# Gates of a dense expert layer applied to two blocks at once, and built two steps sooner

## The chip, the cores and the metric

The kernel runs on one core of a Trainium2 chip. The metric is the device time of one execution in microseconds (us); lower is better. A core has a matrix engine (PE; its weight loads are listed as PEld), a vector engine (DVE), a scalar engine (ACT), a general engine (POOL, which here only issues gathers) and a queue engine (SP, which issues the plain loads). They run side by side and are held together by semaphores.

## The reference, cut to what matters

Two transformer blocks are computed one after the other on 512 tokens of width 1024. Each ends in the same kind of layer, a product-key expert layer with 128 x 128 experts, of which every token uses 8 x 16. That layer is where the change lies:

```
expert_id = ...                     # 128 of 16384 experts for a token, expert = first key * 128 + second key
gate = softmax(best_s, axis=-1)
a = einsum('pd,ped->pe', xb, expert_down[ib])
act = gelu(a, approximate=False) * gate
y = einsum('pe,ped->pd', act, expert_up[ib])
```

## The kernel before, in words

There are four tiles of 128 tokens, and each expert layer (there are two, called layer 0 and layer 1 here) treats them in two ways at the same time.

**Tiles 0 and 1 are gathered.** POOL fetches the rows of the experts that a token uses, one row (4 KB) for each of the 128 tokens at a time, so 512 KB a gather. The DVE works on four such gathers at once, a *unit*: a "u" unit takes four dot products (`score_rows`, L1840), a "v" unit adds four weighed rows (`add_rows`, L1860). There are 128 units in a layer, u and v in turn, and a v unit needs the gelu that ACT made of a u unit three places before it (L1223). The gathered rows stand in two rings of six (`ROWS`), one for u and one for v: POOL may issue a gather only when the DVE has used up the row six places before.

**Tiles 2 and 3 are dense.** All 16384 experts are computed for these 256 tokens, in 128 *blocks* of 128 experts (one first key, all second keys). For block e the PE makes the first product (L739), ACT the gelu (L1197), the DVE multiplies by the gates (*weighs* the block, L1793) and the PE makes the second product (L749), which adds up in PSUM. Both tables of a block are loaded by SP, 512 KB each, through rings of four.

**The gates** of the 256 tokens are a mostly empty matrix, built by small matmuls (L775) for a quarter of the first keys at a time: 32 blocks, 64 *batches* of four tokens. A batch needs "hits" (L1207 and L1210 on ACT) and, for every fourth batch, a "spread" of the first keys (L1770 and L1772 on the DVE, `first_keys`). After four batches ACT copies 16 tokens' gates from PSUM into the gate buffer (`copy_gates`, L1217), 16 copies a quarter. The buffer holds one quarter and is reused in place: copy m of quarter q overwrites the places of blocks 2m and 2m + 1 of quarter q - 1, and waits until these have been weighed. A quarter's first block is weighed only when all 16 copies have been made (`ga_copied`).

**The order** is written out by hand. After a stage that builds quarter 0, a loop runs over *steps* e = 0 to 127 on every engine. In step e the PE does the first product of block e + 16 (from e = 8), the second product of block e and then the batches `batches_due(e - 1)` to `batches_due(e)`. ACT makes the gelus of the units of step e - 1, the gelu of block e + 15, the hits for the PE's next step and the copies that are due. The DVE weighs block e + 3, spreads first keys, does a piece of the choice of experts for tile 1 (41 pieces, in the first 51 steps) and runs the units that `units_due(e)` allows. `unit_table` shares the units out over the steps from assumed costs of the PE and the DVE in each step.

Of the kernel before, what the change touches and what calls it, by code (L numbers as in the profile page):

```python
# [11 lines left out]
ALU = mybir.AluOpType  # L12
# [11 lines left out]
NH, TOPK, NKEY = 8, 16, 128  # L24
# [3 lines left out]
ND = len(DENSE) * P  # L28
# [6 lines left out]
WIDES = ND // WIDE  # L35
AHEAD = 16
EARLY = 24
WEIGHED = 3
ZG = 20
RING = 4  # L40
ROWS = 6
# [59 lines left out]
LATER = (QUARTERS - 1) * BATCHES  # L101


def batches_due(e):

    return 0 if e < 0 else min(LATER, 2 * e + 4 + min(4, e // 2))


def spreads_due(e):

    return 0 if e < 0 else -(-batches_due(e + 1) // 4)


def copies_due(e):

    return 0 if e < 0 else min(LATER // 4, (e + 1) // 2 + 1)


def blocks_before(n):
# [4 lines left out]
def pieces_due(e):  # L124

    return min(PIECES, (e + 1) * 5 // 6)
# [7 lines left out]
def unit_table():  # L134

    room = []
    for e in range(NKEY - 2):
        pe = 3.45 * (1 + (EARLY <= e + AHEAD < NKEY)) + 0.37 * (batches_due(e) - batches_due(e - 1))
        other = 0.61 + 1.69 * (spreads_due(e) - spreads_due(e - 1)) + 1.25 * (pieces_due(e) - pieces_due(e - 1))
        room.append((pe, other))  # L140
    share = ((4 * GROUPS - FIRST_UNITS) * 5.15 + sum(v[1] for v in room)) / sum(v[0] for v in room)
    done, table = 0.0, []
    for pe, other in room:
        done += max(0.0, share * pe - other)
        table.append(done)
    return [FIRST_UNITS + round((4 * GROUPS - FIRST_UNITS) * v / done) for v in table]


UNITS = unit_table()


def units_due(e):

    return FIRST_UNITS if e < 0 else UNITS[min(e, len(UNITS) - 1)]
# [45 lines left out]
class Seen:  # L200
# [5 lines left out]
    def next(self, sem, by=1):  # L206
        self.n[sem.name] = self.n.get(sem.name, 0) + by
        self.eng.wait_ge(sem, self.n[sem.name])


def build(nc, a, out, mod_dram, x_dram, two_pi):
    with ExitStack() as ctx:
        def sb(name, cols, dt=F32):
            return ctx.enter_context(nc.sbuf_tensor(name, [P, cols], dt))[:, :]

        def sem(name):
            return ctx.enter_context(nc.semaphore(name))
# [8 lines left out]
        hT = hT_.rearrange("p (k n) -> p k n", k=KC)  # L226
        w_ = sb("w", 2 * KC * SEC)
        wsec = [w_[:, s * KC * SEC:(s + 1) * KC * SEC].rearrange("p (k n) -> p k n", k=KC) for s in range(2)]
        big = sb("big", 64 * 256)
# [10 lines left out]
        def part(base, at_kib, kib, dt=F32):  # L240
            v = base[:, int(at_kib * 256):int((at_kib + kib) * 256)]
            return v if dt == F32 else v.bitcast(dt)
# [22 lines left out]
        hn_, x_ = [v.rearrange("p t d -> p (t d)") for v in (hn, x)]  # L265
# [17 lines left out]
        gates = [gates_.rearrange("p (a i j) -> p a j i", a=QA, i=8), gates_.rearrange("p (j i a) -> p a j i", a=QA, i=8)]  # L283
# [6 lines left out]
        zg_first = [part(x_, n, 1) for n in range(EARLY - AHEAD)]  # L290

        def zg(e):

            return zg_first[e] if e < len(zg_first) else zg_ring[(e - len(zg_first)) % ZG]

        iaT = hT[:, 7, 0:ND]
        second_no = part(hT_, 14, 0.5, BF16)
# [125 lines left out]
        blk_done, blk_gelu = sem("block_multiplied"), sem("block_gelu_ready")  # L423
        blk_ready, blk_summed = sem("block_weighed"), sem("block_summed")
# [928 lines left out]
        def _(dve):  # L1353
# [3 lines left out]
            tt, ts, stt = nc.vector.tensor_tensor, nc.vector.tensor_scalar, nc.vector.scalar_tensor_tensor  # L1357
# [363 lines left out]
            def peer(layer):  # L1721
# [61 lines left out]
                       second_no[:, n * BATCH:(n + 1) * BATCH].unsqueeze(2).to_broadcast(shape), ALU.is_equal)\  # L1783
                        .then_inc(hit_by_vector, 1)

                def weigh_block(e):
                    at = layer * NKEY + e
                    q, j = divmod(e, QA)
                    if j == 0:
                        dve.wait_ge(ga_copied, (layer * QUARTERS + q + 1) * WIDES)  # L1790
                    dve.wait_ge(blk_gelu, at + 1)
                    z = zg(e).rearrange("p (j i) -> p j i", i=8)
                    tt(z, z, gates[q % 2][:, j, :, :], ALU.mult).then_inc(blk_ready, 1)  # L1793

                chooser = tile_experts(1)
                for n in range(BATCHES):
# [3 lines left out]
                        second_keys(n)  # L1800
                    for u in range(first_units(n - 1), first_units(n)):
                        run_unit(layer, u)
                for e in range(WEIGHED):
                    weigh_block(e)
                for e in range(NKEY):
                    if e + WEIGHED < NKEY:
                        weigh_block(e + WEIGHED)
                    for m in range(spreads_due(e - 1), spreads_due(e)):
                        first_keys(1 + m // WIDES, m % WIDES)
                    for _ in range(pieces_due(e - 1), pieces_due(e)):  # L1810
                        next(chooser)
                    for n in range(units_due(e - 1), units_due(e)):
                        run_unit(layer, n)
# [10 lines left out]
            def run_unit(layer, n):  # L1824
                kind, g = unit(n)
                if kind == "u":
                    score_rows(layer, g)
                else:
                    add_rows(layer, g)
                    if g % GROUPS == GROUPS - 1:  # L1830
                        finish_tile(layer, g // GROUPS, y)
# [104 lines left out]
            for h in range(8):  # L1936
# [3 lines left out]
                for j in range(NT):  # L1940
                    n = h * NT + j
# [24 lines left out]
            for n in range(STICKS + LOOK):  # L1966
# [12 lines left out]
                if n < STICKS:  # L1979
                    h, j = n // NT, NT - 1 - n % NT  # L1980
# [13 lines left out]
                if m >= 0:  # L1994
                    h, j = m // NT, NT - 1 - m % NT
# [85 lines left out]
```

## Time and profile before

| | |
|---|---|
| median of 3 runs | 3348.59 us (3344.89 to 3349.8) |
| profiled execution, its own time | 3350.17 us |
| profiled execution, span from first to last instruction | 3348.4 us |
| PE, DVE, ACT, POOL busy | 92%, 74%, 39%, 40% |
| granted clock of the matrix engine, mean | 0.961 |
| steps 0 to 127 of layer 0 | about 710 to 1644 us |
| steps 0 to 127 of layer 1 | about 2402 to 3338 us |

The busy shares are means over stages with different limits, so the steps have to be read by themselves. Times inside the profile count from the span's start. Durations of neighbouring DVE instructions overlap slightly (a start can lie some 0.08 us before the end of the one before).

### The profile page before, as it was taken

What the parts mean: (1) busy time and instruction counts of PE and PEld (TensorE: products, weight loads), DVE (VectorE), ACT (ScalarE), POOL (GpSimd) and SP (SyncE); (2) the same over time, 40 slices, a digit from 0 to 9 for tenths busy, and PEclk for the clock granted to TensorE, in tenths of its full rate; (3) what the DMA queues carried; (4) which work ended last, traced back from release to release, by engine and by line L of the source; (5) the groups of instructions that cost most, each with busy time, mean ns of one, the idle gap of its engine ahead of it and who ended that gap; (6) DMA issues with size and microseconds to landing.
All of it is one profiled execution on the core that took longest, in us unless ns stands there. A gap on an engine that the chain in (4) does not pass through costs nothing. (4 is left out here: it accounts for less than half of the span.)

```text
span 3348.4 us, 46062 instructions
## 1 busy us (share of the span) xinstructions
PE 3096.9 (92%) x16440; PEld 2061.0 (62%) x16440; DVE 2462.3 (74%) x5627; ACT 1311.1 (39%) x3317; POOL 1342.1 (40%) x1040
## 2 busy tenths in 40 slices
PE   7999899789999998989699999997899999999887
PEld 2466488656666666655344554786666666666553
DVE  5874369979799788877721253599888898788777
ACT  3232122476556555500101162224675565555100
POOL 0000000536566677767300000005356567667765
PEclk9999999899999999999899989998899999999999
DMA  8510262869999999999812101527789999999998
GB/s 293 186 51 26 95 226 70 302 221 391 387 372 400 409 398 409 409 409 409 340 56 82 59 11 38 201 70 269 249 341 392 368 399 408 396 409 409 409 409 346
DMA packets 282683, 931.23 MB, mean 278 GB/s; under 512 B 31804, under 2 KB 32460, under 8 KB 281944
## 3 DMA queue, kind: packets, MB, share of 16 engines
q0 software_dynamic: 147840, 536.96, 41.1%
q1 hardware_dynamic: 134616, 391.34, 31.1%
q8 instruction: 131, 2.15, 0.3%
q14 instruction: 96, 0.79, 0.1%
HBM read 921.87 MB, written 6.32 MB: 277 GB/s over the span
## 5 line engine op out<-in xcount | busy, mean ns | idle before, releaser
L739 PE MATMUL psum<-hT,mod 128*128 128x256 f32 x4096 | 983.0, 395 | 56.5 <-ACT big L1197 52.7
L739 PEld LDWEIGHTS psum<-hT,mod 128*128 128x128 f32 x4096 | 791.7, 198 | 182.4 <-issue 76.1
L1207 ACT ACTIVATE levels<-key_numbers,hT 128x128 bf16<-128x128 f32 x1712 | 541.7, 388 | 318.2 <-PE psum L775 318.2
L1860 DVE SCALAR_TENSOR_TENSOR tmp<-w,small,tmp 128x1024 f32<-128x1024 f32 x339 | 435.8, 1285 | 68.1 <-DMA w<-in_peer_up,tmp 32.9
L2035 POOL DMA_INDIRECT w<-in_peer_u,tmp x172 | 237.3, 1380 | 595.0 <-DVEq L1688 457.8
L1840 DVE CUSTOM_DVE_ANT_0 w<-w,hn 128x1024 f32<-128x1024 f32 x342 | 408.8, 1224 | 70.2 <-DMA w<-in_peer_u,tmp 36.6
L2035 POOL DMA_INDIRECT big<-in_peer_down,tmp x86 | 116.1, 1350 | 722.3 <-DVEq L1688 645.2
L749 PE MATMUL psum<-rows,big 128*128 128x512 f32 x768 | 345.4, 593 | 4.1 <-DVE big L1793 4.1
L775 PEld LDWEIGHTS psum<-x,levels 128*128 128x128 bf16 x6144 | 226.7, 101 | 187.6 <-issue 133.2
L775 PE MATMUL psum<-x,levels 128*128 128x32 bf16 x6144 | 238.3, 196 | 70.3 <-issue 30.8
L1223 ACT ACTIVATE small<-small 128x4 f32<-128x4 f32 x128 | 26.3, 205 | 641.3 <-DVE small L1840 641.2
L2035 POOL DMA_INDIRECT w<-in_peer_down,tmp x170 | 231.4, 1361 | 113.9 <-DVE small L1840 70.3
L1210 ACT ACTIVATE levels<-levels 128x512 bf16<-128x512 bf16 x428 | 269.7, 630 | 13.5
L2035 POOL DMA_INDIRECT w<-in_peer_v,tmp x172 | 213.0, 1238 | 136.1 <-DVE tmp L1860 93.7
L2035 POOL DMA_INDIRECT w<-in_peer_up,tmp x170 | 212.3, 1249 | 117.8 <-DVE tmp L1860 74.8
L1860 DVE SCALAR_TENSOR_TENSOR tmp<-big,small,tmp 128x1024 f32<-128x1024 f32 x169 | 217.2, 1285 | 36.0 <-DMA big<-in_peer_v,tmp 17.4
L749 PEld LDWEIGHTS psum<-rows,big 128*128 128x128 f32 x768 | 145.4, 190 | 155.6 <-issue 151.5
L1840 DVE CUSTOM_DVE_ANT_0 big<-big,hn 128x1024 f32<-128x1024 f32 x170 | 204.2, 1224 | 29.7 <-DMA big<-in_peer_down,tmp 15.7
L749 PE MATMUL psum<-tmp,big 128*128 128x512 f32 x384 | 173.1, 593 | 5.5 <-DVE big L1793 5.5
L749 PE MATMUL psum<-srow,big 128*128 128x512 f32 x384 | 172.6, 592 | 0.0
L1217 ACT ACTIVATE big<-psum 128x512 f32<-128x512 f32 x128 | 135.9, 1062 | 63.5 <-PE psum L775 63.3
L1793 DVE TENSOR_TENSOR big<-big 128x256 f32<-128x256 f32 x192 | 115.3, 606 | 54.9 <-ACT big L1217 52.0
(324 smaller groups left out, 4278.7 us busy)
## 6 DMA issues: line engine op xcount, KB each, us to landing
mod<-in_uT SPq DMA_DIRECT2D x256, 512.0 KB, 6.8
rows<-in_peer_v SPq DMA_DIRECT2D x64, 512.0 KB, 6.8
rows<-in_peer_up SPq DMA_DIRECT2D x64, 512.0 KB, 6.8
w<-in_w_in SPq DMA_DIRECT2D x14, 2048.0 KB, 8.3
srow<-in_peer_v SPq DMA_DIRECT2D x32, 512.0 KB
tmp<-in_peer_v SPq DMA_DIRECT2D x32, 512.0 KB
srow<-in_peer_up SPq DMA_DIRECT2D x32, 512.0 KB
tmp<-in_peer_up SPq DMA_DIRECT2D x32, 512.0 KB
```

Source lines behind the costliest of these rows:

```text
L739: last = nc.tensor.matmul(ps[4 + e % 2][:, 0:ND], ub[e % UV][:, k, :], hT[:, k, ND:SEQ], start=k == 0, stop=k == KC - 1)
L749: last = nc.tensor.matmul(y_dense[n][:, c * 512:(c + 1) * 512], zg(e)[:, n * P:(n + 1) * P], vb[e % UV][:, c * 512:(c + 1) * 512], start=e ...
L775: last = nc.tensor.matmul(ps[6 + n // 4 % 2][:, t * QA:(t + 1) * QA], hits[n % HITS][:, j * P:(j + 1) * P], hot[n // 4 % 2][:, r, n % 4, : ...
L1207: last = nc.scalar.activation(hits[n % HITS][:, j * P:(j + 1) * P], keyno, ACT.Abs, bias=nibT[:, n * BATCH + j:n * BATCH + j + 1])
L1210: nc.scalar.activation(hits[n % HITS], hits[n % HITS], ACT.Relu, scale=-1.0, bias=1.0).then_inc(hit_ready, 1)
L1217: nc.scalar.activation(gates[q % 2][:, :, 2 * m:2 * m + 2, :], ps[6 + m % 2].rearrange("p (j i a) -> p a j i", a=QA, i=8), ACT.Copy).then_ ...
L1223: nc.scalar.activation(g8[g % 2], a8[g % 2], ACT.Gelu).then_inc(act_out, 1)
L1793: tt(z, z, gates[q % 2][:, j, :, :], ALU.mult).then_inc(blk_ready, 1)
L1840: nc.vector.tensor_tensor_reduce(out=row, in0=row, in1=hn[:, g // GROUPS, :], scale=1.0, scalar=0.0, op0=ALU.mult, op1=ALU.add, accum_out= ...
L1860: last = stt(y, row, c8[g % 2][:, b:b + 1], y, ALU.mult, ALU.add)
L2035: nc.gpsimd.indirect_dma_start(ring[n % ROWS], None, table, bass.IndirectOffsetOnAxis(idx[:, c:c + 1], 0))\
```

## The change

Four edits. The DVE weighs blocks in pairs: one multiply over 2 x 256 columns where there were two over 256, with the pair e + 4, e + 5 in every even step e in place of block e + 3 in each step. `batches_due` goes on at 2.5 batches a step up to step 16 (before: up to step 8), so that it is four batches, which are two steps, further on from step 16. `copies_due` lets a copy come two steps earlier than that alone would (in step 2m - 4 for copy m once it has caught up, where it was step 2m - 1), bounded by the batches. And the assumed DVE cost of weighing in `unit_table` falls from 0.61 to 0.45, which moves single units between neighbouring steps.

```diff
-WEIGHED = 3
+WEIGHED = 4
...
-    return 0 if e < 0 else min(LATER, 2 * e + 4 + min(4, e // 2))          # batches_due
+    return 0 if e < 0 else min(LATER, 2 * e + 4 + min(8, e // 2))
...
-    return 0 if e < 0 else min(LATER // 4, (e + 1) // 2 + 1)               # copies_due
+    return 0 if e < 0 else min(LATER // 4, e // 2 + 3, batches_due(e + 1) // 4)
...
-        other = 0.61 + 1.69 * (spreads_due(e) - spreads_due(e - 1)) + ...
+        other = 0.45 + 1.69 * (spreads_due(e) - spreads_due(e - 1)) + ...
...
-                def weigh_block(e):
+                def weigh_pair(e):
                     at = layer * NKEY + e
                     q, j = divmod(e, QA)
                     if j == 0:
                         dve.wait_ge(ga_copied, (layer * QUARTERS + q + 1) * WIDES)
-                    dve.wait_ge(blk_gelu, at + 1)
-                    z = zg(e).rearrange("p (j i) -> p j i", i=8)
-                    tt(z, z, gates[q % 2][:, j, :, :], ALU.mult).then_inc(blk_ready, 1)
+                    dve.wait_ge(blk_gelu, at + 2)
+                    z = zg_pair(e)
+                    tt(z, z, gates[q % 2][:, j:j + 2, :, :], ALU.mult).then_inc(blk_ready, 2)
...
-                for e in range(WEIGHED):
-                    weigh_block(e)
+                for e in range(0, WEIGHED, 2):
+                    weigh_pair(e)
                 for e in range(NKEY):
-                    if e + WEIGHED < NKEY:
-                        weigh_block(e + WEIGHED)
+                    if e % 2 == 0 and e + WEIGHED < NKEY:
+                        weigh_pair(e + WEIGHED)
```

`zg_pair(e)` is the view of the two neighbouring gelu buffers of blocks e and e + 1.

The first place is the DVE at the turn from quarter 0 to quarter 1 of layer 0. `gates_copied` is the semaphore `ga_copied`, and L1770 waits for the PE's batches (`gates_multiplied`). Before:

```order
1336 L1793 TENSOR_TENSOR hT<-hT,big 128x256 [waits block_gelu_ready,v_slots_free]
1337 L1770 TENSOR_TENSOR x<-x,hT 128x512 [waits gates_multiplied]
1338 L1772 TENSOR_TENSOR x<-x,tmp 128x512 [waits first_key_step]
1339 L1772 TENSOR_TENSOR x<-x,tmp 128x512 x2
1340 L1602 MATCH_REPLACE mod<-chosen,mod 128x64 [waits first_keys_spread]
1341 L1602 MATCH_REPLACE mod<-chosen,mod 128x64 [waits choice_step]
1342 L1840 ISA big,small<-big,hn 128x1024 [waits u_landed4,choice_step]
1344 L1840 ISA big,small<-big,hn 128x1024 [waits u_landed5]
1346 L1840 ISA w,small<-w,hn 128x1024 [waits u_landed0]
1348 L1840 ISA w,small<-w,hn 128x1024 [waits u_landed1]
1350 L1793 TENSOR_TENSOR big<-big 128x256 [waits block_gelu_ready,gates_copied]
```

And with the change, the same turn:

```order
1320 L1863 TENSOR_TENSOR small<-small,tmp 128x4 [waits gelu_ready,choice_step]
1321 L1872 SCALAR_TENSOR_TENSOR tmp<-w,small,tmp 128x1024 [waits v_landed2,weights_of_group_ready]
1322 L1872 SCALAR_TENSOR_TENSOR tmp<-w,small,tmp 128x1024 [waits v_landed3,v_slots_free]
1323 L1872 SCALAR_TENSOR_TENSOR tmp<-big,small,tmp 128x1024 [waits v_landed4,v_slots_free]
1324 L1872 SCALAR_TENSOR_TENSOR tmp<-big,small,tmp 128x1024 [waits v_landed5,v_slots_free]
1325 L1805 TENSOR_TENSOR big<-big 128x512 [waits gates_copied,block_gelu_ready,v_slots_free]
1326 L1781 TENSOR_TENSOR x<-x,hT 128x512 [waits gates_multiplied]
1327 L1783 TENSOR_TENSOR x<-x,tmp 128x512 [waits first_key_step]
```

The weighing that waits for the copies stood behind the spread and the unit of step 28, as the first row of step 29; now it is the first row of step 28 and stands ahead of that step's spread (in the changed file L1793 is L1805, L1770 is L1781, L1772 is L1783, L1840 is L1852, L1860 is L1872).

The second place is ACT at the same turn: the last copy of quarter 1 (128x32x16) and the first of quarter 2 (128x32x2x8). Before:

```order
574 L1197 ACTIVATE big<-psum 128x256 [waits block_multiplied,block_summed]
575 L1207 ACTIVATE levels<-key_numbers,hT 128x128 [waits gates_multiplied]
577 L1210 ACTIVATE levels<-levels 128x512 [waits spread_step]
578 L1207 ACTIVATE levels<-key_numbers,hT 128x128 [waits gates_multiplied]
580 L1210 ACTIVATE levels<-levels 128x512 [waits spread_step]
581 L1217 ACTIVATE big<-psum 128x32x16 [waits block_weighed,gates_multiplied]
582 L1197 ACTIVATE big<-psum 128x256 [waits block_multiplied,block_summed]
```

And with the change:

```order
567 L1218 ACTIVATE levels<-key_numbers,hT 128x128 [waits gates_multiplied]
569 L1221 ACTIVATE levels<-levels 128x512 [waits spread_step]
570 L1228 ACTIVATE big<-psum 128x32x16 [waits block_weighed,gates_multiplied]
571 L1234 ACTIVATE small<-small 128x4 [waits u_slots_free]
572 L1208 ACTIVATE big<-psum 128x256 [waits block_multiplied,block_summed]
573 L1218 ACTIVATE levels<-key_numbers,hT 128x128 [waits gates_multiplied]
575 L1221 ACTIVATE levels<-levels 128x512 [waits spread_step]
```

The last copy was made in ACT's step 29 and is made in step 26; behind it now stands the gelu of a unit (L1234, L1223 before), as the copies have moved from odd steps to even ones.

## Rows read from the trace of the kernel before

**Rows 1.** The page: busy time of each engine; GB/s in 40 slices.
```profile
PE 3096.9 (92%) x16440; PEld 2061.0 (62%) x16440; DVE 2462.3 (74%) x5627; ACT 1311.1 (39%) x3317; POOL 1342.1 (40%) x1040
...
GB/s 293 186 51 26 95 226 70 302 221 391 387 372 400 409 398 409 409 409 409 340 56 82 59 11 38 201 70 269 249 341 392 368 399 408 396 409 409 409 409 346
```

**Rows 2.** Windows: busy us of PE, PEld, DVE, ACT, POOL; PE clock, DMA share, GB/s.
```profile
910.00:1190.00 280.00, 279.46 (x1734) 192.20 (x1733) 241.11 (x445) 162.10 (x429) 177.29 (x137) 1.00 0.99 389
1190.00:1600.00 410.00, 380.95 (x1884) 252.49 (x1882) 327.54 (x467) 137.31 (x378) 288.29 (x225) 0.97 1.03 409
2600.00:2880.00 280.00, 278.97 (x1746) 191.78 (x1742) 240.29 (x441) 159.81 (x421) 176.46 (x137) 1.00 1.00 390
```

**Rows 3.** Waits (total us, times, longest): whole run; DVE 900 to 1100; DVE from 1240.
```profile
DVE big L1793 <- ACT big L1217: 52.0, 5, 13.2
...
DVE big L1793 <- ACT big L1217: 13.2, 1, 13.2
DVE x L1770 <- PE psum L775: 2.0, 1, 2.0
...
DVE w L1840 <- DMA w<-in_peer_u,tmp: 30.8, 41, 1.3
```

**Rows 4.** Timeline of DVE, steps 28 and 29 of layer 0.
```profile
899.54 0.61 DVE L1793 TENSOR_TENSOR hT<-hT,big 128x256 f32<-128x256 f32 x1
902.12 0.42 DVE L1770 TENSOR_TENSOR x<-x,hT 128x512 bf16<-128x512 bf16 x1 [1.98 <-PE psum L775]
...
921.95 0.60 DVE L1793 TENSOR_TENSOR big<-big 128x256 f32<-128x256 f32 x1 [13.18 <-ACT big L1217]
```

**Rows 5.** Timelines of PE, then ACT, around the same wait.
```profile
901.92 3.70 PE L739 MATMUL psum<-hT,mod 128*128 128x256 f32 x16
...
908.89 0.93 PE L775 MATMUL psum<-x,levels 128*128 128x32 bf16 x24
909.65 3.70 PE L739 MATMUL psum<-hT,mod 128*128 128x256 f32 x16
...
917.39 3.70 PE L739 MATMUL psum<-hT,mod 128*128 128x256 f32 x16
...
917.21 1.28 ACT L1207 ACTIVATE levels<-key_numbers,hT 128x128 bf16<-128x128 f32 x4 [3.37 <-PE psum L775]
918.51 0.63 ACT L1210 ACTIVATE levels<-levels 128x512 bf16<-128x512 bf16 x1
...
920.88 1.04 ACT L1217 ACTIVATE big<-psum 128x512 f32<-128x512 f32 x1
921.72 0.41 ACT L1197 ACTIVATE big<-psum 128x256 f32<-128x256 f32 x1
```

**Rows 6.** Timeline of POOL across the same wait.
```profile
925.84 1.86 POOL L2035 DMA_INDIRECT w<-in_peer_v,tmp  x1 [13.79 <-DVE tmp L1860]
```

**Rows 7.** Short windows at the waits of quarters 1 and 2, columns as in rows 2.
```profile
910.00:940.00 30.00, 30.00 (x174) 20.35 (x173) 17.63 (x41) 15.84 (x45) 12.68 (x10) 1.00 0.79 283
...
1170.00:1180.00 10.00, 10.00 (x67) 6.42 (x66) 9.86 (x14) 4.07 (x12) 6.99 (x6) 1.00 0.95 340
1180.00:1190.00 10.00, 9.46 (x70) 6.82 (x67) 9.79 (x19) 2.98 (x9) 7.38 (x6) 1.00 1.00 386
```

**Rows 8.** Groups by form: out<-in, count, busy us, mean ns.
```profile
L1793 DVE TENSOR_TENSOR big<-big 128x256 f32<-128x256 f32 x192 | 115.3, 606 | 54.9 <-ACT big L1217 52.0
...
L1506 DVE TENSOR_TENSOR tmp<-big 128x256 f32<-128x256 f32 x36 | 15.0, 416 | 0.0
...
L1578 DVE TENSOR_TENSOR hn<-hn,mod 128x512 f32<-128x512 f32 x8 | 5.5, 692 | 0.3
...
L1700 DVE TENSOR_TENSOR tmp<-tmp,small 128x96 f32<-128x96 f32 x8 | 2.7, 332 | 0.3
...
L1655 DVE TENSOR_TENSOR mod<-mod 128x96 f32<-128x96 f32 x8 | 2.1, 258 | 0.3
```

**Rows 9.** Waits from 1180 to 1640, all engines: total us, times, longest.
```profile
PE psum L739 <- ACT big L1197: 24.9, 7, 8.2
```

More of the change, by code:

```diff
@@ L138, in unit_table @@
         pe = 3.45 * (1 + (EARLY <= e + AHEAD < NKEY)) + 0.37 * (batches_due(e) - batches_due(e - 1))
-        other = 0.61 + 1.69 * (spreads_due(e) - spreads_due(e - 1)) + 1.25 * (pieces_due(e) - pieces_due(e - 1))
+        other = 0.45 + 1.69 * (spreads_due(e) - spreads_due(e - 1)) + 1.25 * (pieces_due(e) - pieces_due(e - 1))
         room.append((pe, other))
@@ L294, in zg, with zg_pair @@
             return zg_first[e] if e < len(zg_first) else zg_ring[(e - len(zg_first)) % ZG]
+        def zg_pair(e):
+            n = e if e < len(zg_first) else (e - len(zg_first)) % ZG
+            if e < len(zg_first):
+                v = part(x_, n, 2).rearrange("p (e n) -> p e n", e=2)
+            elif n < 4:
+                v = hT[:, 3 + n:5 + n, 0:ND]
+            else:
+                v = part(big, 16 + n - 4, 2).rearrange("p (e n) -> p e n", e=2)
+            return v.rearrange("p e (j i) -> p e j i", i=8)
         iaT = hT[:, 7, 0:ND]
```

## The prediction

> **What bounds the kernel now.** I read the page first: the PE is busy 92% of the span and the DVE 74%, but the slices of GB/s stand at 409 for long stretches of both layers' steps [rows 1]. So the steps have two limits in turn, and the windows separate them [rows 2]. From 910 to 1190 us the PE has no gap (279.5 of 280 us) and the DMA engines move 389 GB/s; from 1190 to 1600 us the PE has gaps (381 of 410 us) and the DMA moves 409, its ceiling here. Layer 1 repeats the first with 390. In the second stretch the DVE waits for gathered rows again and again, 30.8 us in 41 waits for those u rows alone whose places lie in w [rows 3]. There the bytes still to be moved set the end. A layer can therefore end earlier only if more bytes have been moved before about 1190 us: the stretch before gives away 280 x (1 - 389/409) = 13.7 us of DMA time in layer 0 and 280 x (1 - 390/409) = 13.0 us in layer 1. These 26.7 us are the most that this change could return.
>
> Where is it lost? The list of waits has the DVE waiting 52.0 us in 5 waits for ACT's copy of gates ahead of a weighing [rows 3]. The timeline shows one [rows 4]: the first weighing of quarter 1 starts at 921.95, after 13.2 us without work. The reader is to see the chain behind it [rows 5]: the PE ends the batches of step 28 as it starts the next first product at 917.39, ACT makes two hit batches and then the copy, from 920.88 to 921.9, and the DVE goes on. While the DVE stands still no row is freed, POOL issues nothing for 13.8 us up to 925.84 [rows 6], and the traffic sinks to 283 GB/s over 910 to 940 [rows 7]: 30 x (1 - 283/409) = 9.2 us. At the next quarter the rings were empty before the wait, so the DMA worked on through most of it and lost only 10 x (1 - 340/409) + 10 x (1 - 386/409) = 2.3 us [rows 7]. The remaining 2.2 of the 13.7 us are scattered.
>
> **The wait at a quarter's start.** With the change the last copy stands in ACT's step 26 and the weighing that needs it at the head of the DVE's step 28. It then waits for the PE's batches of step 26, which end where the next product starts, at 901.92 [rows 5], and takes 1.0 us: done at 903.0. The DVE comes to step 28 at 899.54 and would wait 3.5 us, of which 2.0 us are a wait that it has today one row later, ahead of L1770, for the same batches [rows 4]. So 13.2 us shrink to about 1.5 us. What is late next is the PE itself: a spread in an even step e cannot start before the PE has ended step e - 2. The change moves batches and spreads by the same two steps, so this hold stays where it is, and the DVE can be ahead of the PE only as far as before.
>
> **The batches brought forward.** Four more batches fall into steps 9 to 16. Two take 909.65 - 908.89 = 0.76 us of the PE [rows 5], four 1.5 us. The PE is gapless there, so all that follows until the DMA takes over is 1.5 us later, and with it the DVE's hold. Later steps have as many batches less.
>
> **Copies in even steps.** ACT used to find a copy's batches done; now it waits for the PE to end the step. Behind the copy stand a gelu (0.4 us) and two hit batches (each 1.28 + 0.63 us), some 5.3 us with the copy, in a PE step of 909.65 - 901.92 = 7.7 us [rows 5]. The PE needs the gelu only a step later. Cost nothing, under that cover of 2.4 us; if it is gone, each us over is a us of the PE. The copy also waits for a weighing of the same DVE step, not of the one before; where the DVE lags, ACT already waits for the DVE's units of the step before, so I take nothing here too.
>
> **The pair.** No row shows it. Contiguous float32 products take 416 ns for 256 columns and 692 for 512, so 276 per 256 and 140 fixed; the weighing takes 606, 190 more, with gates read 128 bytes apart [rows 8]. If that surplus grows with the columns the pair takes 606 + 466 = 1072 ns and saves 140; if it is paid once the pair takes 692 + 190 = 882 and saves 330. The nearest row decides: 96 columns of gates with a stride cost 332 ns against 258 contiguous, 0.77 ns a column, and 190/256 is 0.74. It grows, so I take 1072. Over 128 pairs the DVE saves 18 us (42 at most, below nothing only if a longer read were slower for each column). It is worth about nothing at the end: in the first stretch the hold by the PE takes it up, in the second the rows.
>
> The Trainium skill (SBUF — State Buffer, section Door 1) says that reads within a 16-byte line are fast and every change of line costs, which speaks against the pair: the stride leaves one float32 a line, so its surplus would double, as in the rows. The Trainium skill (VectorE: DVE Perf Modes, section on the TRN2 errata) gives a fixed cost per instruction, (N + 151)/0.96 ns for a float32 product, and advises 512 elements or more; by that alone a pair would save 157 ns, against 140 by the rows. By either, the end would not move.
>
> **The unit table.** Single units change places between neighbouring steps: two in step 51 and none in 52 become one in each. The DVE reaches step 54 some 2 us later for that: before, step 52 had no unit and ended early.
>
> **The sum.** The second wait's loss comes back whole, since the DMA is at its ceiling from there to the end: 2.3 us a layer. The first wait's does not: by 1100 us the DVE had worked off its delay (from 900 to 1100 it waits for nothing but this copy and 2.0 us for the PE [rows 3]) and then ran into empty rings. Without the wait it stands at the PE's hold, at the same unit, and the only difference is what lies ready in the rings. They hold 12 rows; by my estimate 8 to 9 can lie ready while the DVE works at four, and 2 to 3 while it waits for rows. Six rows of 0.524 MB at 409 GB/s are 1.28 us each, 7.7 us. Less the 1.5 us of the batches, less about 2 us for the shifted unit, 4.2 us. A layer gains 4.2 + 2.3 = 6.5 us, both 13. The profiled execution took 3350.2 us, 1.6 above the median of the runs; from it the sum gives 3337.2, from the median 3335.6. I say **3336.5**.
>
> **The rivals.** *More comes back* (0.08): the rings never fill, and all of the 26.7 us less twice 1.5 returns, 3326 us. For it: the demand of a step with one unit, 3.15 MB in 7.7 us, is already 407 GB/s. Against it: steps 29 to 52 have 0.96 units each. *Little comes back* (0.21): the DVE had caught up, rings fill at once, and the batches and the shifted unit eat the rest; the second wait alone, 4.6 - 3.0, gives 3348, and all from 3343 on counts here. For it: 200 us lie between the first wait and the DMA's reign, and nothing in the trace ties them. *The wait stays* (0.03): the copy, in its new place, is held by something as late (a spread or hits that ACT cannot make in time), 3350. *A slower PE* (0.07) is the one on the other side: the copy in ACT's even steps holds up gelus or hits behind it. It decides once ACT's work behind a copy exceeds the 2.4 us of cover; with 1 us over in each of 44 such steps the PE is 44 us late in a layer, of which 24.9 are waits for gelus that it has today anyway while the DMA sets the pace [rows 9], so 19 us a layer appear: 3350 + 38 - 13 = 3375.
>
> The Trainium skill (DMA: Bandwidth & Descriptors, section Where 436 GB/s comes from) puts loads from HBM at some 358 GB/s for one core of a pair; the 409 of the rows is above it, and the measurement decides. By 358 the steps would be further in the DMA's hands and the same bytes would return more.
>
> **How the numbers follow.** The forecast, 3329 to 3343 us, has 0.61; more 0.08, little 0.21, the wait stays 0.03, a slower PE 0.07. From the bounds (3326 with all, 3348 with the second wait alone) the range for 8 in 10 is 3328 to 3347: outside stay most of "more" (0.05), the slow end of "little" (0.05), the wait that stays and the slower PE. 0.2% of the time is 6.7 us, about what a measurement of this kernel can tell from no change, so faster means under 3341.9 and slower over 3355.3. Of the forecast 0.58 lies under 3341.9, with "more" 0.66; its slow edge of 0.03, "little" and "the wait stays" are the same, 0.27; slower 0.07.
>
> **What would show it.** Right: the DVE's wait for copies ahead of a weighing falls from 52 us to under 10; GB/s at 910 to 940 stays near 400 and the stretch to 1190 averages 395 to 402; the PE keeps steps of 7.7 us; the pair takes 1.05 to 1.1 us; steps of layer 0 end 5 to 8 us sooner. Wrong: new waits of the PE for hits or gelus between 760 and 1100 us; a layer whose first stretch moves more bytes and ends no sooner; or DMA waits of the DVE already before 1000 us, which would mean that the rings never fill and more comes back.

## The result, and the profile after

| | |
|---|---|
| before, runs beside it | 3350.21 us (3344.89 to 3357.72, 7 runs) |
| changed | 3370.1 us (3361.51 to 3374.43, 7 runs) |
| ratio | 1.0057, 95% interval 1.0044 to 1.0069 |

The change makes the kernel 0.57% slower, about 19 us; 3336.5 was forecast, with 3328 to 3347 as the range. The profiled execution took 3370.1 us, its span is 3368.3.

The page of the changed kernel, busy times and GB/s in 40 slices:

```profile
PE 3095.6 (92%) x16440; PEld 2059.4 (61%) x16440; DVE 2454.6 (73%) x5499; ACT 1307.5 (39%) x3317; POOL 1329.8 (39%) x1040
...
GB/s 294 182 51 26 105 214 70 302 221 329 408 385 382 409 409 409 409 409 409 346 56 81 45 25 38 199 65 264 256 292 401 388 379 409 409 409 409 409 409 349
```

Beside [rows 1] two things stand out. The dips at the waits for copies have shrunk (385 where it was 372 in the twelfth slice, 409 where it was 398 in the fifteenth), though the thirteenth slice fell from 400 to 382. But the slice in which the steps get under way has sunk in both layers: 329 where it was 391, and 292 where it was 341. Windows of the changed kernel, columns as in [rows 2]:

```profile
750.00:910.00 160.00, 153.64 (x1010) 104.97 (x1009) 134.34 (x285) 105.55 (x284) 94.92 (x72) 0.99 0.93 356
910.00:940.00 30.00, 30.00 (x189) 20.45 (x188) 25.01 (x57) 16.92 (x47) 18.26 (x16) 1.00 1.01 398
910.00:1190.00 280.00, 280.00 (x1735) 192.46 (x1734) 244.71 (x438) 164.52 (x438) 182.47 (x141) 1.00 1.01 393
...
1190.00:1600.00 410.00, 380.02 (x1893) 253.81 (x1892) 319.72 (x435) 132.05 (x365) 272.52 (x220) 0.97 1.03 409
2440.00:2600.00 160.00, 152.82 (x1041) 102.83 (x1039) 129.91 (x284) 108.94 (x290) 88.00 (x68) 1.00 0.90 343
```

The kernel before, in the two stretches that no row has shown yet:

```profile
750.00:910.00 160.00, 159.94 (x1015) 109.42 (x1012) 139.47 (x307) 100.70 (x268) 99.67 (x79) 1.00 1.00 390
...
2440.00:2600.00 160.00, 159.48 (x1004) 108.98 (x1005) 140.35 (x307) 101.02 (x267) 99.25 (x78) 1.00 1.00 388
```

At the quarter's start all went nearly as forecast: 398 GB/s over 910 to 940 where it was 283 [rows 7], and 393 against 389 up to 1190 [rows 2]. The loss is in the stretch ahead of it, where the prediction had put nothing but 1.5 us for four batches: the PE, gapless before, stands still for 6.4 us there and for 7.2 us in layer 1, and 34 and 45 GB/s less are moved.

What it waits for is in the timelines of PE and then ACT, steps 11 to 16 of layer 0:

```profile
784.10 1.31 PE L786 MATMUL psum<-x,levels 128*128 128x32 bf16 x36
786.47 3.69 PE L750 MATMUL psum<-hT,mod 128*128 128x256 f32 x16 [1.06 <-ACT big L1208]
...
803.17 3.69 PE L750 MATMUL psum<-hT,mod 128*128 128x256 f32 x16 [0.69 <-ACT big L1208]
...
812.53 3.69 PE L750 MATMUL psum<-hT,mod 128*128 128x256 f32 x16 [1.48 <-ACT hT L1208]
...
829.60 3.69 PE L750 MATMUL psum<-hT,mod 128*128 128x256 f32 x16 [1.06 <-ACT hT L1208]
...
785.06 1.05 ACT L1228 ACTIVATE big<-psum 128x512 f32<-128x512 f32 x1 [5.00 <-PE psum L786]
785.91 0.41 ACT L1208 ACTIVATE big<-psum 128x256 f32<-128x256 f32 x1
```

ACT stands for 5.00 us ahead of a copy (L1228) until the PE has ended its batches (L786), copies for 1.05 us, then makes a block's gelu (L1208), and only then can the PE begin its next first product (L750), which overwrites the PSUM bank that the gelu reads. The two engines take turns.

Why only here follows from the tables. In step 9 the new `copies_due` asks for 7 copies, so 28 batches, but the PE has made only `batches_due(9)` = 26 by then and reaches 29 in step 10: the bound of a copy is `batches_due(e + 1)`, the batches of the PE's *next* step. So it is in steps 9, 11, 12 and 14, and the four stalls above are two steps behind each. From step 16 on `e // 2 + 3` copies need exactly the batches of step e, and no stall is left. Before, steps 1 and 3 alone asked too much, when ACT has no gelu of a block in its steps yet; with the change 1, 3, 4, 6 and 7 do. There hits come late instead: the PE's batches (L786) wait for ACT's hits (L1221). In the waits from 705 to 770 us of the changed kernel (total, times, longest):

```profile
PE psum L786 <- ACT levels L1221: 6.1, 7, 1.3
```

against 4.7 us in 6 before. With them goes a second price. Right behind two of them starts the second product of step 6, and it takes 5.38 us where the same product takes 3.68 us before:

```profile
753.08 0.55 PE L786 MATMUL psum<-x,levels 128*128 128x32 bf16 x12 [0.79 <-ACT levels L1221]
754.91 0.55 PE L786 MATMUL psum<-x,levels 128*128 128x32 bf16 x12 [1.28 <-ACT levels L1221]
755.30 5.38 PE L760 MATMUL psum<-tmp,x 128*128 128x512 f32 x8
```

The granted clock over 750 to 760 us is 0.83 in the changed kernel and 1.00 before: after these two waits the PE ran for a part of the stretch at the lower of its two levels (1.2 and 2.4 GHz). Waits of the whole run, and the new weighing among the groups by form (count, busy us, mean ns):

```profile
ACT big L1228 <- PE psum L786: 382.9, 97, 11.8
...
DVE x L1781 <- PE psum L786: 94.2, 34, 6.1
...
L1805 DVE TENSOR_TENSOR big<-big 128x512 f32<-128x512 f32 x96 | 101.6, 1058 | 13.2 <-ACT big L1228 8.9 <-issue 1.0
```

The DVE's waits for copies ahead of a weighing fell from 52.0 us [rows 3] to 8.9; its waits for the PE's batches ahead of a spread rose from 59.0 to 94.2. A part of that is the forecast hold by the PE and a part the PE's lateness in the ramp: e1 below, without the stalls, has 74.7. The pair takes 1058 ns.

### The profile page after: what moved, and what is told of

Read it like the earlier page. It is cut to its first block and busy times, and to the rows that moved or that the text cites. A ratio compares the mean times of both kernels' runs of the same rounds, so it can differ in the third digit from the quotient of the medians.

```text
span 3368.3 us, 45972 instructions
## 1 busy us (share of the span) xinstructions
PE 3095.6 (92%) x16440; PEld 2059.4 (61%) x16440; DVE 2454.6 (73%) x5499; ACT 1307.5 (39%) x3317; POOL 1329.8 (39%) x1040
## 5 line engine op out<-in xcount | busy, mean ns | idle before, releaser
L750 PE MATMUL psum<-hT,mod 128*128 128x256 f32 x4096 | 978.2, 394 | 68.1 <-ACT big L1208 57.8
L750 PEld LDWEIGHTS psum<-hT,mod 128*128 128x128 f32 x4096 | 788.3, 197 | 195.8 <-issue 90.6
L1872 DVE SCALAR_TENSOR_TENSOR tmp<-w,small,tmp 128x1024 f32<-128x1024 f32 x339 | 435.6, 1285 | 75.0 <-DMA w<-in_peer_up,tmp 33.7
L1852 DVE CUSTOM_DVE_ANT_0 w<-w,hn 128x1024 f32<-128x1024 f32 x342 | 408.9, 1222 | 79.2 <-DMA w<-in_peer_u,tmp 39.3
L786 PEld LDWEIGHTS psum<-x,levels 128*128 128x128 bf16 x6144 | 226.1, 101 | 189.7 <-issue 133.0
L786 PE MATMUL psum<-x,levels 128*128 128x32 bf16 x6144 | 237.7, 196 | 74.5 <-issue 32.4
L1228 ACT ACTIVATE big<-psum 128x512 f32<-128x512 f32 x128 | 137.1, 1071 | 392.8 <-PE psum L786 382.9
L1221 ACT ACTIVATE levels<-levels 128x512 bf16<-128x512 bf16 x428 | 270.1, 631 | 13.6
L1872 DVE SCALAR_TENSOR_TENSOR tmp<-big,small,tmp 128x1024 f32<-128x1024 f32 x169 | 217.2, 1285 | 36.7 <-DMA big<-in_peer_v,tmp 16.5
L1852 DVE CUSTOM_DVE_ANT_0 big<-big,hn 128x1024 f32<-128x1024 f32 x170 | 204.1, 1222 | 39.0 <-DMA big<-in_peer_down,tmp 19.5
L1234 ACT ACTIVATE small<-small 128x4 f32<-128x4 f32 x128 | 25.9, 202 | 530.4 <-DVE small L1852 530.4
L737 PE MATMUL psum<-hT,w 128*128 128x256 f32 x640 | 144.8, 379 | 0.0
```

The lines of the kernel that those rows point to most:

```text
L737: last = nc.tensor.matmul(bank[:, 0:2 * P], w[:, k, c * P:(c + 1) * P], hT[:, k, tokens], start=k == 0, stop=k == KC - 1)
L750: last = nc.tensor.matmul(ps[4 + e % 2][:, 0:ND], ub[e % UV][:, k, :], hT[:, k, ND:SEQ], start=k == 0, stop=k == KC - 1)
L786: last = nc.tensor.matmul(ps[6 + n // 4 % 2][:, t * QA:(t + 1) * QA], hits[n % HITS][:, j * P:(j + 1) * P], hot[n // 4 % 2][:, r, n % 4, : ...
L1221: nc.scalar.activation(hits[n % HITS], hits[n % HITS], ACT.Relu, scale=-1.0, bias=1.0).then_inc(hit_ready, 1)
L1228: nc.scalar.activation(gates[q % 2][:, :, 2 * m:2 * m + 2, :], ps[6 + m % 2].rearrange("p (j i a) -> p a j i", a=QA, i=8), ACT.Copy).then_ ...
L1852: nc.vector.tensor_tensor_reduce(out=row, in0=row, in1=hn[:, g // GROUPS, :], scale=1.0, scalar=0.0, op0=ALU.mult, op1=ALU.add, accum_out= ...
```

## The experiments

The same kernel before ran beside all of them; it took 3352.6 us on the chip of the four runs e1 to e4, 3367.1 on that of f1 to f4 and 3365.9 on that of g1 to g4, so all are given as ratios to it. To see where time goes, the table has the time from the second product of one step to that of another in layer 0, read from the PE's timelines (before: 710.02, 758.14, 820.39 and 1620.42 for steps 0, 8, 16 and 122).

| kernel | ratio [95%] | steps 0-8 | 8-16 | 16-122 |
|---|---|---|---|---|
| before | 1 | 48.1 | 62.3 | 800.0 |
| changed | 1.0057 [1.0044, 1.0069] | 50.1 | 68.3 | 797.8 |
| e1, copies bounded | 1.0000 [0.9991, 1.0009] | 46.4 | 63.4 | 797.9 |
| e2, two products for the pair | 1.0044 [1.0030, 1.0058] | 49.5 | 68.3 | 798.1 |
| e3, pair alone | 0.9990 [0.9981, 0.9999] | 48.0 | 62.3 | 801.7 |
| e4, old batches, copies bounded | 1.0023 [1.0013, 1.0033] | 46.4 | 62.3 | 804.4 |
| f4, copy behind the next gelu | 1.0029 [1.0018, 1.0039] | 53.3 | 63.4 | 799.4 |
| g2, old batches, new copies | 1.0577 [1.0562, 1.0592] | 53.2 | 71.6 | 889.3 |
| f1, e1 and 3 units more | 0.9934 [0.9921, 0.9948] | 46.5 | 63.4 | 796.1 |
| f2, before and 3 units more | 0.9963 [0.9951, 0.9976] | 49.7 | 63.1 | 793.1 |
| f3, e3 and 3 units more | 0.9926 [0.9912, 0.9940] | 50.3 | 62.3 | 790.7 |
| g1, f3 with two products | 0.9921 [0.9907, 0.9934] | 51.0 | 62.3 | 791.5 |
| g3, f3 and units sooner | 0.9939 [0.9925, 0.9952] | 47.2 | 62.3 | 797.2 |
| g4, changed and 3 units more | 1.0000 [0.9991, 1.0009] | 53.9 | 70.1 | 793.3 |

The times of steps come from one profiled execution each, and those of the f and g kernels from other chips. The added units change nothing in the program of steps 0 to 8, so each of its forms was measured several times there, over both layers: 46.4 to 46.5 us with bounded copies (e1, e4, f1), 47.0 to 51.0 with the old tables (before, e3, f2, f3, g1, g3) and 49.4 to 53.9 with the change's copies (changed, e2, f4, g2, g4). The last two overlap, so a single difference of under 4 us between them can be scatter; that bounded copies are faster is not.

**e1: copies ask only for batches of their own step.**

```diff
-    return 0 if e < 0 else min(LATER // 4, e // 2 + 3, batches_due(e + 1) // 4)
+    return 0 if e < 0 else min(LATER // 4, e // 2 + 3, batches_due(e) // 4)
```

> The changed kernel with one term altered: a copy of gates is due in a step only when the batches of that same step of the PE complete it (bounded by batches_due(e), not batches_due(e + 1)). From step 16 on nothing differs. Theory A, the ramp: in steps 9 to 16 ACT's copy waits for batches that the PE makes only a step later, the gelu behind it is late, and the PE's next first product waits for it. Then the PE's steps 8 to 17 go back to 7.7 us, the 8 us that the PE lost between 750 and 850 us come back but for some 1.5 us for the four batches more, and in layer 1 as well: 3370 - 2 x 6.5 = 3357 if nothing else comes free, and down to 3345 if the stall that vanished at the quarter's start then shows as a gain. Rival B, the loss is the four earlier batches themselves or the DVE's pairs, and ACT's waits only show it: the steps stay at 8.1 to 9.4 us and the time within 3 us of 3370. Rival C, the PE's lateness is made good or lost elsewhere (full rings): steps of 7.7 us, but the time over 3364.

The ratio falls from 1.0057 to 1.0000, so the whole loss, some 19 us, hangs on this one term. Steps 0 to 16 take 109.8 us where the changed kernel needed 118.4; layer 1 shows the same, 109.8 for 117.8 (2404.77 to 2514.54 against 2415.71 to 2533.54). That is 16.6 of the 19 us. Steps 16 to 122 take as long in both. Theory A holds, and by the steps' times also its count: the four stalls are 4.3 us of the 4.9 that steps 8 to 16 lost. In steps 0 to 8 the changed kernel waits 6.1 us for hits where e1 waits 3.5, and its product of 5.38 us takes 3.68 in e1.

The spans of the profiled executions of before and changed differ by 19.9 us, of which 4.7 lie ahead of step 0, where e1, e2 and e4 have the changed kernel's program and begin step 0 at 712.98, 708.30 and 707.06 us against its 714.76. That part is scatter of single executions. From step 0 of layer 0 to step 0 of layer 1 it is 1691.9 us before, 1701.0 changed and 1691.8 in e1.

So the loss is gone in e1, but nothing is *won*. The windows of e1 say where the gain goes:

```profile
750.00:910.00 160.00, 159.28 (x1046) 109.72 (x1043) 137.95 (x294) 108.08 (x289) 97.43 (x76) 1.00 0.98 378
910.00:940.00 30.00, 30.00 (x191) 20.82 (x190) 29.29 (x65) 16.86 (x47) 19.76 (x17) 1.00 1.03 408
...
940.00:1100.00 160.00, 160.00 (x1000) 109.89 (x999) 142.21 (x268) 95.11 (x252) 99.97 (x76) 1.00 1.00 386
```

and the kernel before over the last of these stretches:

```profile
940.00:1100.00 160.00, 160.00 (x1003) 110.58 (x1000) 155.46 (x302) 98.60 (x257) 105.69 (x86) 1.00 1.02 404
```

In us of the DMA at 409 GB/s, e1 wins 30 x (408 - 283)/409 = 9.2 over 910 to 940, loses 160 x (404 - 386)/409 = 7.0 over 940 to 1100 and 160 x (390 - 378)/409 = 4.7 over 750 to 910, and wins 90 x (409 - 398)/409 = 2.4 from 1100 to 1190: nothing in the sum. After 940 the kernel before works off what the stall held up, with the DVE busy 97% of the time. e1 has nothing to work off; from 940 to 1100 its DVE waits 13.0 us in 5 waits for the PE's batches ahead of a spread, where before had no wait in this stretch. The bytes follow from the tables: steps 29 to 52 hold 22 units (32 due at step 28, 54 at step 52) of 2.10 MB and 24 blocks of 1.05 MB, 71.3 MB in 24 PE steps of (917.39 - 901.92)/2 = 7.74 us [rows 5], which is 384 GB/s. With a gapless PE the steps ask for no more, stall or not.

**e4 and g2: the batches as before, with bounded copies and with the new rule.** Both have `min(4, e // 2)` in `batches_due` again.

> The changed kernel with the batches as before (2.5 a step only up to step 8) and copies bounded by the batches of the same step. So pairs and early copies stay, without the four batches forward and without the coupling of the ramp. Theory A: the PE's steps 8 to 17 are 7.7 us, the PE has no gap to 1190 us; the DVE's wait at the head of step 28 is for the batches of the PE's step 28, so it returns at 12 to 16 us and the traffic sinks to under 300 GB/s there as before: 3350 plus or minus 4, no better than the kernel before. If the four earlier batches cost more than their 1.5 us a layer, this kernel is faster than the one with bounded copies by more than 4 us; if they are what buys the stall, it is slower than that one by 4 us or more.

> The changed kernel with the four batches forward taken back alone, its rule for copies left. Then the copy of every odd step from 9 on asks for batches that the PE makes one step later, not only four of the steps 9 to 16: 26 such steps up to step 60, where the PE sets the pace. Theory A, by which the changed kernel lost 4.9 us to four such steps between steps 8 and 16, so 1.2 each: 26 x 1.2 = 31 us in a layer, of which the DMA, its share unused before, makes nothing good; 3350 + 62 = 3412, at the least 3385. If such a copy costs the PE nothing by itself and the changed kernel lost its time to the batches, this kernel is at 3350 to 3362 like the one with old batches and bounded copies.

e4 has no stall in its steps 8 to 16 (62.3 us), but is 0.23% slower than before, 3360.8 us where 3350 plus or minus 4 was expected: with the pair at the head of step 28 the DVE waits 24.5 us there for a copy, where 12 to 16 were expected. So the four batches are not what costs; they buy 0.23% (e1 against e4). That they do so by shortening this wait, to 4.4 us in e1, is argued. g2 is the suspected cost in a large dose, since old batches leave every odd step's copy one step short. Its page of waits:

```profile
ACT big L1228 <- PE psum L786: 751.7, 98, 12.4
...
PE psum L750 <- ACT big L1208: 156.2, 72, 6.6
```

and its PE, two neighbouring steps of the same size:

```profile
847.72 3.69 PE L750 MATMUL psum<-hT,mod 128*128 128x256 f32 x16 [1.71 <-ACT hT L1208]
...
855.45 3.70 PE L750 MATMUL psum<-hT,mod 128*128 128x256 f32 x16
...
864.82 3.69 PE L750 MATMUL psum<-hT,mod 128*128 128x256 f32 x16 [1.48 <-ACT big L1208]
```

Every second step is held. The sign and the place are as expected and the size is not: 62 us more were expected, and 1.0577 is some 190. The stall is dearer than I took it: from step 8 to 60 two steps take (1242.3 - 770.1)/26 = 18.2 us against 15.5, so 2.7 for each copy where I took 1.2. From 940 to 1100 us the PE stands for 16.9 of 160 us, which is 1.9 us in two steps, and its granted clock is 0.97 where it is 1.00 before. And it does not end at step 60. The DMA moves only 363 GB/s from 1190 to 1600, so there the PE still sets the pace.

**f4: the changed kernel, with ACT's copy behind the next step's gelu.**

```diff
                         block_gelu(layer, e + AHEAD - 1)
+                    for m in range(copies_due(e - 2), copies_due(e - 1)):
+                        copy_gates(layer, 1 + m // WIDES, m % WIDES)
                     for n in range(batches_due(e) if e else 0, batches_due(e + 1)):
                         hit_batch(layer, 1 + n // BATCHES, n % BATCHES)
-                    for m in range(copies_due(e - 1), copies_due(e)):
-                        copy_gates(layer, 1 + m // WIDES, m % WIDES)
```

> The changed kernel with all its tables, and only ACT's order altered: the copies that are due in a step come behind the block gelu of the next step, ahead of its hits, where they stood ahead of it. A copy in the ramp still waits for batches that the PE makes a step later. Theory A says that the loss lay in the gelu behind that copy, for which the PE's next first product waits: then the PE's steps 8 to 17 are 7.7 us and the time is that of the kernel with bounded copies, 3353 plus or minus 4. If it was the hits behind the copy that made the PE late, the steps stay above 8 us and the time above 3362.

Half a hit. Steps 8 to 16 go to 63.4 us, e1's value, though ACT still waits for those batches (18.9 us from 750 to 845, 26.0 in the changed kernel): there it was the gelu behind the copy. But only half of the loss in time is back. In steps 0 to 8 there is no block's gelu to put ahead of a copy, and a copy that waits stands ahead of the hits of the PE's next batches, as in the changed kernel. These steps take 53.3 us and hold 6.6 us of waits for hits and two second products of 5.38 us, one more of them than in the changed kernel. A kernel with only the hits moved was not run, so how much of this part is theirs stays argued. The 3.2 us more than the changed kernel's 50.1 can't be told from scatter: g4, with the changed kernel's order, takes 53.9.

**e2, e3 and g1: the pair.** e3 is the kernel before with pairs e + 2, e + 3 (`WEIGHED = 2`) and all old tables; e2 and g1 make two products at the pair's place:

```diff
-                    z = zg_pair(e)
-                    tt(z, z, gates[q % 2][:, j:j + 2, :, :], ALU.mult).then_inc(blk_ready, 2)
+                    for i in range(2):
+                        z = zg(e + i).rearrange("p (j i) -> p j i", i=8)
+                        tt(z, z, gates[q % 2][:, j + i, :, :], ALU.mult).then_inc(blk_ready, 1)
```

> The changed kernel with the pair's product made as two products of 256 columns at the same place, each announcing its block. If the one operation saves what the rows after the change give (two of 606 ns against one of about 1.07 us, some 140 ns a pair, 18 us of the DVE in all) and the DVE is never what the end waits for, the time stays within 4 us of the changed kernel's 3370. If the fused operation itself is part of the loss (the PE gets block e + 4 half a microsecond later, or a slower read), the time falls by more than 5 us. If the DVE's time does count, it rises by up to 18 us, to 3388.

> The kernel before with the pair alone: batches, copies and the unit table as before, and the pair e + 2, e + 3 in every even step (two steps further on would need a copy that ACT makes only after the DVE's step). Theory A (the loss is the ramp of the copies): no new waits between 750 and 850 us, the PE's steps 8 to 17 at 7.7 us, the end at 3350 plus or minus 5; the first quarter's weighing comes one step later than before, so the DVE's wait for the copy there shrinks from 13.2 us to 5 or less of the PE's lead, and up to 8 us a layer could come back, 3334 at the best. Rival (the pair is the loss: it hands over blocks too late for the PE or reads slowly): the PE waits for weighings in the stretch to 1190 us and the time is 3360 or more.

> The fastest kernel so far (pair alone with three units more, 0.74% faster than before) with the pair's product made as two products at the same place in the program. It tells the one operation from the later place, one and two blocks further on in an even step. The DVE was busy for 93 to 97% between 940 and 1100 us in these kernels. If the place and the units make the gain, the ratio to before stays at 0.993 plus or minus 0.001. If the operation's saving, some 140 ns a pair or 9 us a layer, counts now that the DVE has more to do, it rises towards 0.996, which the kernel before reached with the same units.

All three came out within what was expected of them. The one operation is worth nothing that can be measured: 1.0044 against 1.0057, and 0.9921 against 0.9926, with intervals that overlap. e3 is 0.1% faster than before at most, and it has the first wait halved (6.4 us for 13.2) with the PE's steps as before: half of the stall gone, and almost nothing won by it.

**f1, f2, f3, g3 and g4: more units early.** If the table is what holds the traffic down, it has to be lifted. Each has up to three units more due, rising from step 12 to 50 and given back up to step 120 (57 due at step 52 where it was 54); g3 has up to four, rising from step 7 to 26:

```diff
-    return FIRST_UNITS if e < 0 else UNITS[min(e, len(UNITS) - 1)]
+    if e < 0:
+        return FIRST_UNITS
+    more = round(3 * min(1.0, max(0, e - 12) / 38, max(0, 120 - e) / 70))
+    return min(4 * GROUPS, UNITS[min(e, len(UNITS) - 1)] + more)
```

> The changed kernel with bounded copies, and up to three units more due from step 12 to 50 (57 of the 128 are due at step 52 where it was 54), given back up to step 120. Theory D: without the stall the DVE runs into the end of what the unit table lets it do and is held by the PE's batches (9.3 us from 910 to 1000, 3.7 to 1100 in the kernel with bounded copies), and from 940 to 1100 us the traffic is 385 GB/s because the steps ask for no more; so the stall cost nothing that the table would have allowed. With three units of 2.1 MB more by step 50 the traffic there goes to 400 or more and the DMA's share of a layer, (409 - 385) / 409 x 160 = 9 us at most, comes back for the most part: 3353 - 2 x 4 to 8 = 3338 to 3345. Rival E: the DVE has no room for them (93% busy from 1000 to 1100), weighs late and the PE waits: 3353 to 3370. Rival F: the DMA's bytes are not what sets the end: 3353 plus or minus 3.

> The kernel before, not changed but for the same three units more by step 50. It still has the wait of 13.2 us at the quarter's start, and its DVE is busy for 97% of 1000 to 1100 us. Theory D: here the stall does cost, since the DVE has no room to make it good; it gains less than the kernel with bounded copies and the same units, 0 to 6 us: 3344 to 3353. If it gains as much as that one (under 3343), the early copies and batches were not needed for the gain; if it is slower than 3356, the DVE is the bound once more is asked of it.

> The pair alone (old batches, copies in odd steps, pair e + 2, e + 3 in step e) with the same three units more by step 50. It was 3349 without them, with a wait of 6.4 us at the quarter's start. Theory D: between the other two, with its stall half as long: 3338 to 3347. Rivals as before: 3350 or more if the DVE becomes the bound.

Windows of f1, then of f3:

```profile
910.00:940.00 30.00, 30.00 (x189) 20.45 (x188) 26.46 (x57) 17.90 (x49) 18.13 (x14) 1.00 1.03 409
...
940.00:1100.00 160.00, 160.00 (x981) 110.06 (x980) 150.29 (x288) 96.49 (x252) 110.85 (x83) 1.00 1.03 409
```

```profile
910.00:1190.00 280.00, 279.92 (x1732) 191.90 (x1731) 251.51 (x442) 167.15 (x439) 191.87 (x147) 1.00 1.03 407
1190.00:1600.00 410.00, 388.47 (x1928) 257.18 (x1927) 320.06 (x437) 136.42 (x372) 283.74 (x218) 0.97 1.03 409
```

Theory D holds. By the sum above, 24 units in steps 29 to 52 of f1 make 406 GB/s. Measured are 408 to 409 in f1 from 910 us on, with a PE that has no gap up to 1190, and the kernel with bounded copies goes from 1.0000 to 0.9934. f2 shows that the table alone gives 0.37% (I had expected 0.2% at most), with the stall still there (320 GB/s over 910 to 940). From f2 to f1 and f3 there are 0.29% and 0.37% more, 10 and 12 us: about the 13 us that I had put on the stalls, and they come only once the table asks for the bytes. That reading is argued, since f1 and f3 differ from f2 in more than the stall. The longest wait of the DVE ahead of a weighing from 900 to 1100 us is 11.4 us in f2, 5.2 in f3 and 2.9 in f1; f3 was expected between the other two and is not behind f1 (0.9926 against 0.9934, the intervals overlap), so the gain does not follow the length of the stall step by step.

> The changed kernel as it is, with the three units more by step 50. By theories A and D together the two costs add up: the ramp's copies still make the PE 8 us later in each layer, the units give back what they gave the kernel with bounded copies (0.9934 against 1.0000): ratio 1.0057 - 0.0066 = 0.999 plus or minus 0.0015. If the DMA, now at its ceiling, makes the PE's lateness harmless (the steps after 16 are then no longer set by the PE), the ratio is 0.995 or less.

> The fastest kernel so far with the units put forward sooner: four more by step 26 (36 due at step 28 where it was 33), the same from step 44 on. Its traffic from 750 to 910 us was 387 GB/s, from 910 on 408. Theory D: what is unused there, (409 - 387) / 409 x 160 = 8.6 us, comes back in part: ratio 0.989 to 0.992. Rival: the DVE, which there also chooses experts and spreads keys, weighs late and the PE waits: ratio 0.993 to 1.0.

g4 lands where the sum of both effects puts it, 1.0000 where 0.999 was expected: the ramp's cost is not hidden by a busy DMA, because there the DMA isn't busy (340 GB/s over 750 to 910). g3 is not faster than f3, and lands in its rival's range, but not by late weighings: the traffic from 750 to 910 stays at 385 and the PE gets gaps there instead (156.04 us busy of 160, and 151.84 in layer 1). The longest, 3.2 us ahead of 873.58 (6.0 us in layer 1), is a wait for a block's gelu. ACT had stood 12.6 us for the DVE, which was late with a u unit, ahead of that unit's gelu, and the block's gelu stands behind it. The first product after the gap takes 6.37 us in place of 3.70, with a granted clock of 0.66 over 870 to 880 us, so it ran in part at the lower level.

f3 and g1 are the fastest, 0.74% and 0.79% under the kernel before (3340.3 and 3339.7 us, on chips where that takes 3367.1 and 3365.9). They have neither the earlier batches nor the earlier copies of the change.

## Why the prediction was wrong

- **The step that failed** is "The PE needs the gelu only a step later. Cost nothing, under that cover of 2.4 us". I worked it out for the steady state, around step 26, from [rows 5], and there it is true: from 910 to 1190 the PE is gapless. In the ramp, steps 1 to 14, the copy asks for batches that come a step later still; then there is no cover, and what stands behind the copy is on the PE's path. e1 measured it: 19 us in place of nothing, 16.6 of them in steps 0 to 16 of the two layers. I had both tables at hand, and comparing four times the copies with the batches of each step would have shown it.
- **The rival** "a slower PE" (0.07) named the engines and the chain, a copy in ACT's steps that holds up the gelu, and the sign. Its condition and size were not right: it is not the amount of work behind the copy, in 44 steps, but four steps (and hits in five before) in which the copy waits for the step ahead; 8 us a layer, not 19. That its 3375 lies near the measured 3370 is luck: it is 38 us of loss less 13 of gain, where some 19 of loss and no gain were measured.
- **The gain**, 13 us, did not come either, and this would have made the forecast miss by itself: e1, with all of the change but the fault, is at 1.0000. The term of 4.2 us for the first wait rested on "the only difference is what lies ready in the rings". The windows of e1 show in its place that the kernel before made most of its 9.2 us good by a DVE at 97%, up to the same limit of units per step. I had put the demand of these steps at 0.96 units and 407 GB/s for one; their table holds 22 in 24, and 384 GB/s. "Little comes back" (0.21), with 3348, was the nearest of the rivals to e1's about 3350. For the second wait 2.3 us a layer were put down as whole; 1100 to 1190 did rise from 398 to 409 in e1, 2.4 us, and as much was lost earlier.
- **More that could be returned.** The 26.7 us were rightly counted as DMA time not used, but the stalls alone do not account for it. Taking stalls away by itself returned nothing (e1) to 0.1% (e3), the table by itself some 12 us (f2), and both together 22 and 25 us (f1 and f3).
- **What held.** The wait for copies fell from 52 us to 8.9 (under 10 was forecast), 13.2 us at the first one to 4.4 (1.5 forecast); 398 GB/s over 910 to 940 (near 400); the hold by the PE ahead of spreads took the wait's place; the pair takes 1058 ns (1072 forecast), worth nothing at the end. The average over 910 to 1190, 393, stayed under the 395 to 402 that I gave as a sign of being right. Of the signs of being wrong the first came, new waits of the PE for gelus between 760 and 1100.
- The Trainium skill (SBUF — State Buffer, section Door 1) spoke against the pair; by its rule the surplus of the strided read would double. The 1058 ns agree: the surplus over a contiguous product is 366 ns for 512 columns and 190 for 256. It made no difference to the time, as said.
- **What stays open**: why e1 and f1 move only 378 and 371 GB/s from 750 to 910 where e3 and f3 move 385 and 387. They differ in the batches, the spreads, the copies and the unit table's weights at once.

## What to carry to other kernels

When a table sets how far ahead an engine may run, check each consumer's table against its producer's at every step, the ramp above all: a steady state with cover says nothing of the steps in which the numbers catch up. An engine that works in order hands a wait on to all that stands behind it; here the PE paid for ACT's copies (changed, g2) and for ACT's wait on the DVE (g3), and each gap of the PE could cost a slower clock on top. Before a stall is priced by the traffic lost in it, look at whether the engine works the delay off afterwards; if it does, up to a limit that a table sets, the table is what to change, and here the stall seemed to be worth something only after that.

## What the runs showed of the hardware

A product of 512 float32 columns with one operand read at a stride of 128 bytes takes 1058 ns, with 256 columns 606 [rows 8]; so 452 for 256 columns more, against 276 when contiguous. A gap of 3.2 us of the PE in g3 was followed by a product of 6.37 us in place of 3.70, at a granted clock of 0.66 over the ten us around it, while four gaps of 0.69 to 1.48 us in the changed kernel's steps 11 to 16 left the products behind them at 3.69 us; in g4 the one behind a gap of 1.48 us took 5.38. The DMA held 407 to 409 GB/s from 910 to 1600 us in f3 beside a PE that was busy for 668 of these 690 us. The same kernel before took 3353 us on one chip and 3367 and 3366 on two others, 0.4% apart, nearly as much as the effect studied here, so only runs on one chip can be compared.
